# An expert layer on one core: gate and up weights fetched in pieces of 8 KB per partition, the gathered rows turned by sixteen small products instead of four transposes

## What is computed

```
def hierarchical_moe(hn, w_group, b_group, w_router, b_router, w_gate, w_up, w_down):
    ...
    for grp in range(N_GROUPS):
        a = jnp.einsum("nd,edf->nef", t, w_gate[grp])
        u = jnp.einsum("nd,edf->nef", t, w_up[grp])
        act = jax.nn.silu(a) * u * gates[:, grp, :, None]
        y = y + jnp.einsum("nef,efd->nd", act, w_down[grp])
```

## Time and profile before

| | |
|---|---|
| median of 3 runs | 1124.71 us (1123.81 to 1128.26) |
| the profiled execution, own time | 1123.33 us |
| its span in the profile | 1121.4 us |
| mean granted clock of PE over the span | 0.984 |
| PE busy | 1043.3 us (93%) |
| DVE, ACT, POOL busy | 406.7, 253.9, 157.4 us |
| DMA over the span | 277 MB, 247 GB/s |
| expert stages, about | 348 to 581 us and 870 to 1099 us of the span |

### The profile page before, as it was taken

How to read it: one execution, slowest core, us unless ns; L and a number is a source line. 1 busy time by engine, 2 the same in 40 slices (tenths; PEclk the granted TensorE clock), 3 DMA queues, 4 the chain that set the end, 5 groups by cost and what they waited for, 6 DMA issues and landing times.

```text
span 1121.4 us, 13304 instructions
## 1 busy us (share of the span) xinstructions
PE 1043.3 (93%) x5232; PEld 556.2 (50%) x5232; DVE 406.7 (36%) x1131; ACT 253.9 (23%) x669; POOL 157.4 (14%) x168
## 2 busy tenths in 40 slices
PE   5999999999998999999788998899998999999886
PEld 3344644455455555554434647536455555555442
DVE  3122721344154422332135216548136332233225
ACT  3122720244011111110012216537111111111002
POOL 2000000000001233223201000000100223322220
PEclk9999999999998999999899999999999999999898
DMA  9521207955218999999989310023524999999986
GB/s 322 215 91 68 75 2 196 224 218 188 100 42 333 368 411 411 410 410 410 408 341 359 116 75 1 10 75 152 192 113 154 351 408 411 411 410 410 409 350 229
DMA packets 80063, 277.00 MB, mean 247 GB/s; under 512 B 13646, under 2 KB 17854, under 8 KB 71290
## 3 DMA queue, kind: packets, MB, share of 16 engines
q1 hardware_dynamic: 68464, 256.56, 60.1%
q0 software_dynamic: 11536, 19.58, 5.0%
HBM read 261.94 MB, written 30.44 MB: 261 GB/s over the span
## 4 chain that ended last, share of the span: by engine, by line
PE 79%; DMA 8%; SPq 4%; DVE 4%; ACT 3%; issue 2%; POOL 0%; POOLq 0%; DVEq 0%; ACTq 0%
PE bank L1023 16%; PE bank L810 13%; PE bank L900 10%; PE bank L822 9%; PE bank L1036 8%; PE bank L841 5%; DMA W<-in_moe_w_up 4%; PE bank L1012 3%; SPq L436 3%; PE bank L852 3%; PE bank L868 2%; PE bank L1030 2%; PE bank L1171 2%; DMA hnT<-expert_rows 1%; PE bank L934 1%
## 5 line engine op out<-in xcount | busy, mean ns | idle before, releaser
L1023 PE MATMUL bank<-W,K 128*64 128x256 f32 x640 | 157.1, 402 | 21.4 <-DMA W<-in_moe_w_up 19.4
L1024 PE MATMUL bank<-W,K 128*64 128x256 f32 x640 | 157.2, 402 | 0.0
L810 PE MATMUL bank<-hnT,W 128*128 128x512 f32 x336 | 145.1, 593 | 0.8 <-ACT hnT L1262 0.8
L1023 PEld LDWEIGHTS bank<-W,K 128*64 128x64 f32 x640 | 89.1, 144 | 72.5 <-DMA W<-in_moe_w_up 22.3
L1693 DVE SCALAR_TENSOR_TENSOR PT<-bank,small,PT 64x256 f32<-64x256 f32 x64 | 31.4, 491 | 257.6 <-ACT PT L1332 257.6
L642 POOL DMA_INDIRECT K<-rows,small x64 | 65.8, 1028 | 399.4 <-DVE K L1713 275.9
L810 PEld LDWEIGHTS bank<-hnT,W 128*128 128x128 f32 x336 | 63.5, 190 | 80.5 <-issue 79.5
L1036 PE MATMUL bank<-D,PT 128*64 128x512 f32 x208 | 100.3, 604 | 0.7 <-ACT PT L1336 0.7
L1038 PE MATMUL bank<-D,PT 128*64 128x512 f32 x208 | 100.3, 604 | 0.0
L1024 PEld LDWEIGHTS bank<-W,K 128*64 128x64 f32 x640 | 89.1, 144 | 0.0
L1332 ACT ACTIVATE PT<-bank,small 64x256 f32<-64x256 f32 x64 | 29.9, 468 | 240.7 <-PE bank L1024 238.0
(11 more groups left out here) (249 smaller groups left out, 1506.8 us busy)
## 6 DMA issues: line engine op xcount, KB each, us to landing
D<-in_moe_w_down SPq DMA_DIRECT2D x52, 1024.0 KB, 22.5
W<-in_moe_w_gate SPq DMA_DIRECT2D x40, 1024.0 KB
W<-in_moe_w_up SPq DMA_DIRECT2D x40, 1024.0 KB
hnT<-in_moe_w_down SPq DMA_DIRECT2D x12, 1024.0 KB, 15.5
W<-in_e_w_in SPq DMA_DIRECT2D x5, 2048.0 KB
expert_rows<-K SPq DMA_DIRECT2D x2, 4096.0 KB, 34.7
Q<-in_moe_w_gate SPq DMA_DIRECT2D x6, 1024.0 KB
Q<-in_moe_w_up SPq DMA_DIRECT2D x6, 1024.0 KB
```

What stands on the lines that cost most here:

```text
L810: last = nc.tensor.matmul(b[:, :], w[:, k, 128 * fb:128 * fb + 128], hnT[:, k, :], start=(k == 0), stop=(k == KD - 1))
L1023: nc.tensor.matmul(bank[2 + e2][0:64, 0:256], xt, w[0][:, at:at + 256], start=first, stop=end)
L1024: last = nc.tensor.matmul(bank[2 + e2][64:128, 0:256], xt, w[1][:, at:at + 256], start=first, stop=end)
```

## The change

Three things, which only work together:

1. Feature d now stands at partition p, piece k with d = 8p + k, so that gate and up are each one piece of 8 KB per partition, as down already is (lines 108, 109, 435 of the new program).
2. To bring the rows into that order, the first halves (partitions 0 to 63 of `Xg`) must end on partitions 0 to 63 and the second halves on 64 to 127. So `transpose_rows` makes, for each of 8 pieces, two products with a 64 x 64 block of the identity: one with partitions 0 to 63 into PSUM partitions 0 to 63, one with 64 to 127 into 64 to 127. The stationary operand takes every eighth column of `Xg`. These are plain float32 products, not transposes.
3. `gate_up` and `rows_in` read the new order. Counts and sizes there stay: 16 products of 256 columns, one DVE instruction on 128 x 512.

In `further_tiles` a single transpose into an unused bank is put ahead; its loop is not entered.

```diff
-    wg_v = [moe_w_gate[l].rearrange("g e (h p k) f -> (g e) p h (k f)", h=2, p=128) for l in range(2)]
-    wu_v = [moe_w_up[l].rearrange("g e (h p k) f -> (g e) p h (k f)", h=2, p=128) for l in range(2)]
+    wg_v = [moe_w_gate[l].rearrange("g e (p k) f -> (g e) p (k f)", p=128) for l in range(2)]
+    wu_v = [moe_w_up[l].rearrange("g e (p k) f -> (g e) p (k f)", p=128) for l in range(2)]
...
             def load_half(lay, e, part):
                 gate_up, _, done, _ = expert_slot(lay, e)
-                sp.dma_start(gate_up[part].rearrange("p (h x) -> p h x", h=2), (wg_v, wu_v)[part][lay][e])\
+                sp.dma_start(gate_up[part], (wg_v, wu_v)[part][lay][e])\
                   .then_inc(done[0], 16 if slot_of(e) == 6 or not part else 32)
...
             def transpose_rows(e2, src):
-                for k in range(4):
-                    last = nc.tensor.transpose(bank[e2][:, 128 * k:128 * k + 128],
-                                               src.rearrange("p (x k) -> p k x", k=4)[:, k, :], ident)
+
+                for k in range(KD):
+                    for half in range(2):
+                        at = slice(64 * half, 64 * half + 64)
+                        last = nc.tensor.matmul(bank[e2][at, 64 * k:64 * k + 64],
+                                                src.rearrange("p (x k) -> p k x", k=KD)[at, k, :], ident[at, at],
+                                                start=True, stop=True)
                 return last
 
             def gate_up(e2, w):
 
-                for half in range(2):
-                    for k in range(4):
-                        xt = XT[e2][:, 128 * k + 64 * half:128 * k + 64 * half + 64]
-                        at = 1024 * half + 256 * k
-                        first, end = half + k == 0, half + k == 4
-                        nc.tensor.matmul(bank[2 + e2][0:64, 0:256], xt, w[0][:, at:at + 256], start=first, stop=end)
-                        last = nc.tensor.matmul(bank[2 + e2][64:128, 0:256], xt, w[1][:, at:at + 256],
-                                                start=first, stop=end)
+                for k in range(KD):
+                    xt = XT[e2][:, 64 * k:64 * k + 64]
+                    at = 256 * k
+                    nc.tensor.matmul(bank[2 + e2][0:64, 0:256], xt, w[0][:, at:at + 256],
+                                     start=(k == 0), stop=(k == KD - 1))
+                    last = nc.tensor.matmul(bank[2 + e2][64:128, 0:256], xt, w[1][:, at:at + 256],
+                                            start=(k == 0), stop=(k == KD - 1))
                 return last
...
-                nc.vector.tensor_tensor(XT[e2].rearrange("p (k h t) -> p k h t", k=4, h=2),
-                                        bank[e2][:, :].rearrange("p (k h t) -> p k h t", k=4, h=2),
-                                        rows_gain.rearrange("p h k -> p k h").unsqueeze(3).to_broadcast([128, 4, 2, 64]),
-                                        ALU.mult).then_inc(done, 1)
+                nc.vector.tensor_tensor(XT[e2].rearrange("p (k t) -> p k t", k=KD),
+                                        bank[e2][:, :].rearrange("p (k t) -> p k t", k=KD),
+                                        rows_gain.unsqueeze(2).to_broadcast([128, KD, 64]), ALU.mult).then_inc(done, 1)
```

More of the change, by code:

```diff
@@ L244, in trunk @@
         gidx, sidx = small[:, 388:420].bitcast(i32), small[:, 420:452].bitcast(i32)
-        router_gain, rows_gain = small[:, 452:460], small[:, 460:468].rearrange("p (h k) -> p h k", h=2)
+        router_gain, rows_gain = small[:, 452:460], small[:, 460:468]
         rec = small[:, 468:500].bitcast(i32)
@@ L427, in load_expert @@
                 for v, part, count in ((wg_v[lay], 0, 16), (wu_v[lay], 1, 32)):
-                    dst = gate_up[part].rearrange("p (h x) -> p h x", h=2)
-                    sp.dma_start(dst, v[bass.ds(w, 1), :, :, :].rearrange("a p h x -> (a p) h x"))\
+                    sp.dma_start(gate_up[part], v[bass.ds(w, 1), :, :].rearrange("a p x -> (a p) x"))\
                       .then_inc(done, count)
@@ L638, in routing @@
                                allow_slow_non_contiguous=True).then_inc(s_small, 16)
-                pool.dma_start(rows_gain, ffn_norm[lay].rearrange("(h p k) -> p h k", h=2, p=128)).then_inc(s_small, 16)
+                pool.dma_start(rows_gain, ffn_norm[lay].rearrange("(p k) -> p k", p=128)).then_inc(s_small, 16)
             def gather(lay, dst, idx_col, done):
@@ L1078, in further_tiles @@
                         pe.wait_ge(o_["gathered"], o * 16 + 16)
+                        nc.tensor.transpose(bank[4][:, 0:128], Xg[0][:, 0:128], ident)
                         transpose_rows(0, Xg[0]).then_inc(o_["xt"], 1)
```

## The result

The changed kernel takes 1179.35 us, the median of 4 runs (1176.53 to 1183.34), against 1124.96 (1123.81 to 1128.26) for the kernel before: a ratio of 1.0486, 95% interval 1.046 to 1.0513. It is **slower by 54 us**, and outside the predicted range. One run in this document, 1254.30 us of the version with eight transposes, was in a slower state with a mean granted clock of 0.847, and its ratio leaves it out. The profiled execution took 1176.53 us, with a span of 1174.7 against 1121.4.

A forecast was written before the change was run, and what follows sets the result against it. PE, racing full DMA in both expert stages, was taken to set the end. Slack of 14.0 and 12.6 us against +0.40 us per expert gave -1.0 us from 1123.33, so 1124 us as a median; range 1116 to 1158.

The forecast's parts named there:

- the slack: How much slower PE could be in an expert stage without harm: 14.0 us in the first, 12.6 us in the second.
- the slope: How total time follows the turning of one expert's rows: 0.1 us more there is 6.4 us in all.
- the set: PE's instructions that turn one expert's gathered rows: forecast at 1.08 us instead of 0.68, +0.40 us per expert.
- PE's side: Shift of an expert stage's end if PE sets it: -1.2 us in the first stage, +0.2 us in the second.
- The larger pieces: Gate and up weights loaded in 8 KB pieces: -3.9 us per stage on DMA's side, bounds -1.7 and -4.4.
- Halves side by side: In the turning of the rows, passes on the two row halves of PE's array overlap, making 16 rounds of 32 passes.
- the pace: Time per round in the turning of the rows, 0.059 us; also time per expert, 6.98 us instead of 6.58.
- a round: In the turning of the rows, one pass of each row half with its weight load, overlapped: 0.059 us, 16 per set.
- the sum: Both expert stages together, the later of PE's side and DMA's side (-2.7 us each stage) counting: -1.0 us in all.
- Spaced weight loads show: Rival: loading every eighth column lengthens each round of the turning to 0.088 us, set 1.52 us, time 1152 us; chance 0.12.
- The serial rival: Row halves writing the same PSUM bank do not run side by side: set 2.03 us, time 1185 us; chance 0.15.
- The signs named in advance: Wrong if passes start one by one (2 us set), expert pace stays, or PE waits 5 us for weights in a stage.

The follow-up runs named there:

- the version with eight transposes: Changed kernel with eight transposes of 64 spaced columns over all 128 partitions instead of sixteen products, VectorE moving the upper half: 1127.01 us, ratio 1.0022 against kernel before.

## Why the prediction was wrong

- **What bounds the kernel, the slack, the slope**: right. The prediction said that 0.1 us on the set is 6.4 us, that PE's side decides, and that DMA's gain is then worth only room. With columns side by side the set was 1.07 against the 1.08 forecast, the expert 6.99 against 6.98, and the time 1125.5 against 1124.
- **The larger pieces**: right in kind and near in size: -3.9 us per stage forecast, about -3 measured alone, inside the bounds of -1.7 and -4.4. In the changed kernel they gave nothing, as forecast, because PE decides.
- **Halves side by side**: right. Leaving one half out changed nothing. The Trainium skill's rule (TensorEngine Tiling (Array Packing), "Gotcha 1: PSUM Pressure") that different row tiles cannot access one bank at the same time did not hold in these runs: 32 passes into one bank took 1.15 us, where the 0.055 of 64 columns each would make 1.76 one after the other.
- **The step that failed** is the pace, the 0.059 us of a round: "Loads of 128 spaced columns follow each other in (0.56 - 0.208)/3 = 0.117 us; 64 columns are half, 0.059." The row shows transposing loads, and the new instruction is an f32 product. The product's load of columns 16 bytes or more apart costs about 1.85 ns each, twice as much, so 0.119 for 64. And 0.117 need not be the pace of a load at all: with eight transposes, loads of half as many columns still came every 0.116 us, beneath passes of 128 columns. That a product needs two loads was counted rightly, in the 16 rounds. Fifteen steps at 0.06 too little are 0.90 us, and the last load's own longer duration (212 against 135 ns side by side) is the other 0.08. (2.06 - 1.08) x 64 = 63 us is the whole miss of the sum, less the 8.4 us that came back, most of it at the ends of the stages.
- **A row that could have warned**: the kernel before shows that the two kinds of load have different prices. For 128 columns side by side it is 190 ns in a product (L810) and 141 in a transpose (L852). The prediction compared only transposes with each other.
- **The rivals.** "Spaced weight loads show" named the right cause and had it at 0.088 a round: it added half of the 67 ns by which a spaced transposing load is longer, though what was in doubt was another kind of load. The serial rival had nearly the right set, 2.03 us, and so a time (1185) close to the measured one, for a reason that is false. A forecast that rested on it would have been right by luck. Its chance of 0.15 was almost the only part of the forecast at this place, and the range stopped short of it at 1158.
- **The signs named in advance**: a set of 2 us and passes that start one by one were to mean "wrong". The set took 2.06 us and the pace was 7.98 instead of 6.98, but a set of 2 us could not tell the two slow rivals apart; that took the runs with the columns side by side and with one half. PE's waits for up weights fell under 2 us as forecast. Here that says only that PE had become the slower side, by far more than was meant. The sign for the larger pieces, over 412 GB/s at share 1 with gate and up alone, was not read: the stretch compared here, 416 GB/s at share 1.02, brings down weights as well.

## What to carry to other kernels

A duration read for a transpose is not the price of a product that does the same job: in f32 the product has two passes and two loads for one, and in these runs its round doubled once the stationary columns were 16 bytes or more apart. A pace read from a pipeline belongs to whichever part is the slower one, here perhaps the pass: halving it for a load assumes that the load was. When an edit changes both how many matrix instructions there are and how their operand is strided, price the load from a row with the same instruction and the same stride; where no such row exists, keep the doubled value inside the range. And when an edit lengthens a step that stands once in a loop of 64, multiply before anything else: here the 3 us per stage that the transfers gave stood against 30 that the turning took.

## What the runs showed of the hardware that I had not expected

- f32 product, weight load of 64 columns: 0.058 us a round at 4 bytes, 0.060 at 8, 0.119 at 16 and at 32. A step, not a slope.
- A transposing load of 64 columns at 32 bytes fits into a round of 0.055 us, where the product's takes 0.119. That it pays nothing for the distance is not shown: for 128 columns its duration is 208 ns at 16 bytes and 141 side by side. Beneath its pass that hardly shows.
- Row halves, and transposes of 64x64 in row halves, run side by side; the first kind into one bank, the second into two banks on the same partitions.
- With tiles of 128 rows by 64 columns like those of its neighbours, the same set of sixteen products costs some 0.36 us less an expert than with tiles of 64 by 64 (7.62 against 7.98 us). What part of that is the change of the tile's shape is open.
